# First layer of a two-layer decoder step: keys of the first sample batch during the prompt attention, difference-head norms by one root per 128 tokens

## What is computed

```python
diff = pb[:, :, 0] - lam * pb[:, :, 1]
ob = jnp.einsum('bhqk,bkhe->bqhe', diff.astype(vb.dtype), vb)
ob = rms_norm(ob, subln0) * (1.0 - LAMBDA_INIT)
return jnp.concatenate([oa.reshape(B, Q, -1), ob.reshape(B, Q, -1)], axis=-1)
```

## Time and profile before

| | us |
|---|---|
| median of three runs | 2104.91 (2103.43 to 2105.34) |
| the profiled execution's own time | 2101.7 |
| its span | 2099.8 |
| PE busy | 1811.7 (86%) |
| DVE busy | 992.5 (47%) |
| ACT busy | 565.1 (27%) |
| granted TensorE clock, mean | 0.91 |

### The profile page before, as it was taken

How to read it: one execution, slowest core, us unless ns; L and a number is a source line. 1 busy time by engine, 2 the same in 40 slices (tenths; PEclk the granted TensorE clock), 3 DMA queues, 4 the chain that set the end, 5 groups by cost and what they waited for, 6 DMA issues and landing times. The chain is left out here.

```text
span 2099.8 us, 30563 instructions
## 1 busy us (share of the span) xinstructions
PE 1811.7 (86%) x11582; PEld 1447.3 (69%) x11590; DVE 992.5 (47%) x1748; ACT 565.1 (27%) x1051; POOL 98.8 (5%) x89
## 2 busy tenths in 40 slices
PE   5998784888799999999989775666788999999999
PEld 4786452554479998899778632343446899789987
DVE  3456577444443222322246859998333422222222
ACT  3322352333322221122132331332222322112221
POOL 1312021000000000000001200000000000000000
PEclk8999896999899999999989955888789999999999
DMA  5232002999522322232215200000454222232221
GB/s 167 71 121 83 23 1 91 356 348 359 185 63 68 90 69 79 78 87 76 78 40 150 51 2 9 1 1 6 145 162 110 60 82 80 68 83 80 80 76 61
DMA packets 176381, 201.56 MB, mean 96 GB/s; under 512 B 21531, under 2 KB 130779, under 8 KB 176283
## 3 DMA queue, kind: packets, MB, share of 16 engines
q1 hardware_dynamic: 171242, 193.96, 28.9%
q10 hardware_dynamic: 4960, 6.05, 0.8%
q0 software_dynamic: 80, 0.26, 0.0%
HBM read 191.02 MB, written 9.22 MB: 95 GB/s over the span
## 5 line engine op out<-in xcount | busy, mean ns | idle before, releaser
L206 PE MATMUL ps<-feat_lo,w_hi 128*128 128x288 f32 x1408 | 418.7, 297 | 8.9 <-DVEq L1818 8.9
L208 PE MATMUL ps<-feat_hi,w_hi 128*128 128x288 f32 x1408 | 418.4, 297 | 0.0
L207 PE MATMUL ps<-feat_hi,w_lo 128*128 128x288 f32 x1408 | 418.2, 297 | 0.0
L188 DVE TENSOR_TENSOR w_lo<-w_raw,w_hi 128x2048 fp32r<-128x2048 f32 x96 | 220.1, 2293 | 386.2 <-ACT w_hi L182 386.1
L182 ACT ACTIVATE w_hi<-w_raw 128x2048 fp32r<-128x2048 f32 x96 | 183.8, 1914 | 366.4 <-PE ps L214 337.1
L206 PEld LDWEIGHTS ps<-feat_lo,w_hi 128*128 128x128 f32 x1408 | 267.4, 190 | 10.1 <-DVEq L1818 10.1
L207 PEld LDWEIGHTS ps<-feat_hi,w_lo 128*128 128x128 f32 x1408 | 267.5, 190 | 0.0
L208 PEld LDWEIGHTS ps<-feat_hi,w_hi 128*128 128x128 f32 x1408 | 267.3, 190 | 0.0
L206 PE MATMUL ps<-w_lo,feat_hi 128*128 128x512 f32 (+1 forms) x448 | 179.8, 401 | 18.7 <-DVE feat_lo L1707 9.4
L207 PE MATMUL ps<-w_hi,feat_lo 128*128 128x512 f32 (+1 forms) x448 | 176.4, 394 | 0.0
L208 PE MATMUL ps<-w_hi,feat_hi 128*128 128x512 f32 (+1 forms) x448 | 176.4, 394 | 0.0
(11 more groups left out here) (272 smaller groups left out, 2532.2 us busy)
## 6 DMA issues: line engine op xcount, KB each, us to landing
s_kslot<-in_cache_l_k_dram SPq DMA_DIRECT2D x64, 512.0 KB, 7.7
s_vslot<-in_cache_l_v_dram SPq DMA_DIRECT2D x64, 512.0 KB, 7.3
w_raw<-in_w_gate_dram SPq DMA_DIRECT2D x44, 512.0 KB, 4.0
w_raw<-in_w_up_dram SPq DMA_DIRECT2D x44, 512.0 KB, 5.2
w_raw<-in_w_in_dram SPq DMA_DIRECT2D x18, 1024.0 KB, 5.2
w_raw<-in_w_down_dram SPq DMA_DIRECT2D x16, 1024.0 KB, 5.0
s_kslot<-in_cache_l_k_dram SPq DMA_DIRECT2D x64, 128.0 KB, 2.2
s_vslot<-in_cache_l_v_dram SPq DMA_DIRECT2D x64, 128.0 KB, 2.6
```

Of the source, the lines that this page charges most:

```text
L188: dve.tensor_tensor(self.K.w_lo[:, n % 2, :], self.K.w_raw[:, n % 2, :], self.K.w_hi[:, n % 2, :].bitcast(F32), ALU.subtract).then_inc(sel ...
L206: pe.matmul(out, lhs[0], rhs[1], start=start, stop=False)
L207: pe.matmul(out, lhs[1], rhs[0], start=False, stop=False)
L208: return pe.matmul(out, lhs[0], rhs[0], start=False, stop=stop)
```

## The change

In the first layer only:

- `EarlyKeys`: SP loads the first batch's eight key pages while `a0` runs, into the space where `kt` will be (`kt0` over `feat_hi`, and `w_raw`). Its eight semaphores are `s0`'s `k_in`. To have semaphores enough, those of the earlier blocks are cleared by POOL at the start of `a0` and given back behind it.
- In `s0` the first batch's keys are turned out of that space, and the turned keys go to `vslot` (`kt_first`). So the first value pages wait until the first scores are done (`scored` at 4), and all eight of the second batch's key pages are asked for ahead of them instead of four.
- `HeadNorm` takes the place of both norms. ACT squares; PE multiplies 128 squared columns as the stationary operand by one column of ones, so that a sum per token lies in a partition (16 matmuls with one output column for the prompt); DVE scales 128 x 16 numbers, POOL takes the power -0.5, PE spreads each column back over 128 partitions (transpose of a broadcast column), and DVE applies it, reading PSUM. In `s0` the sums stand between the two halves of the first batch's units, the spreading and applying behind `scores(0)` and ahead of the loop. The sample heads' norm is done the same way inside `o0`: sums ahead of token tile 1, spreading ahead of tile 3; the sample columns are split after it.
- The block `sample_subln` is gone.

```diff
-def prompt_attention(nc, K, tag, q_at, k_at, v_at, gates, mask, mixed, sample_top=None):
+def prompt_attention(nc, K, tag, q_at, k_at, v_at, gates, mask, mixed, sample_top=None, early_keys=None, retired=()):
...
-        if any(mixed(p) for p in range(PAIRS)):
+        if retired or any(mixed(p) for p in range(PAIRS)):
             @block.gpsimd
             def _(pool):
+                for lo, hi in number_runs(retired):
+                    pool.sem_clear(range(lo, hi))
...
-        if sample_top is not None:
-            @block.sync
-            def _(sp):
+        @block.sync
+        def _(sp):
+            if early_keys is not None:
+                early_keys.load(sp)
+            if sample_top is not None:
                 sample_top.store(sp)
...
-class PromptSubln:
+class EarlyKeys:
+    def __init__(self, K, tag, cache_k):
+        self.K, self.cache_k = K, cache_k
+        self.k_in = [K.sem(f"{tag}_k_in_{j}") for j in range(N_PAGES)]
+        both = (K.kt0[:, :], K.w_raw.rearrange("p a n -> p (a n)"))
+        width = cache_k.shape[2]
+        self.pages = [both[j // 4][:, (j % 4) * width:(j % 4 + 1) * width] for j in range(N_PAGES)]
+    def load(self, sp):
+        for j in range(N_PAGES):
+            page = sp.value_load(self.K.pages[0:1, j:j + 1], min_val=0, max_val=self.cache_k.shape[0] - 1)
+            sp.dma_start(self.pages[j], self.cache_k[ds(page, 1), :, :].rearrange("a k d -> (a k) d"))\
+              .then_inc(self.k_in[j], 16)
+class HeadNorm:
+    def __init__(self, K, name, views, squares, sums, banks):
+        self.K, self.views, self.squares, self.banks = K, views, squares, banks
+        names = ("squared", "summed", "mean_ok", "rstd_ok", "spread", "normed")
+        self.S = {x: K.sem(f"{name}_{x}") for x in names}
+        self.n = len(views)
+        self.per = squares[0].shape[1] // P
+        self.sums = sums[:, 0:self.n * self.per]
+        self.norm = K.lams[:, 0:2, 0:self.n * self.per]
+    def square(self, act):
+        for k in range(self.n):
+            dst = self.squares[k]
+            if len(self.views[k].shape) == 3:
+                dst = dst.rearrange("p (h n) -> p h n", h=self.views[k].shape[1])
+            act.activation(dst, self.views[k], ACT.Square).then_inc(self.S["squared"], 1)
+    def sum_up(self, pe):
+        pe.wait_ge(self.S["squared"], self.n)
+        for k in range(self.n):
+            for x in range(self.per):
+                c = k * self.per + x
+                ins = pe.matmul(self.sums[:, c:c + 1], self.squares[k][:, x * P:(x + 1) * P], self.K.c("ones")[:, 0:1],
+                                start=True, stop=True)
+        ins.then_inc(self.S["summed"], 1)
+    def mean(self, dve):
+        dve.wait_ge(self.S["summed"], 1)
+        dve.tensor_scalar(self.norm[:, 0, :], self.sums, 1.0 / P, EPS, ALU.mult, ALU.add).then_inc(self.S["mean_ok"], 1)
+    def root(self, pool):
+        pool.wait_ge(self.S["mean_ok"], 1)
+        pool.tensor_tensor(self.norm[:, 1, :], self.norm[:, 0, :], self.K.c("minus_half")[:, 0:self.n * self.per],
+                           ALU.pow).then_inc(self.S["rstd_ok"], 1)
+    def bank(self, k):
+        return self.banks[k % len(self.banks)]
+    def spread(self, pe):
+        pe.wait_ge(self.S["rstd_ok"], 1)
+        for k in range(self.n):
+            if k >= len(self.banks):
+                pe.wait_ge(self.S["normed"], k - len(self.banks) + 1)
+            for x in range(self.per):
+                c = k * self.per + x
+                ins = pe.transpose(self.bank(k)[:, x * P:(x + 1) * P], self.norm[:, 1, c:c + 1].to_broadcast([P, P]),
+                                   self.K.c("ident"))
+            ins.then_inc(self.S["spread"], 1)
+    def apply(self, dve):
+        for k in range(self.n):
+            view, scale = self.views[k], self.bank(k)[:, 0:self.per * P]
+            if len(view.shape) == 3:
+                scale = scale.rearrange("p (h n) -> p h n", h=view.shape[1])
+            dve.wait_ge(self.S["spread"], k + 1)
+            dve.scalar_tensor_tensor(out=view, in0=view, scalar=self.K.subln_col8[:, 0:1], in1=scale,
+                                     op0=ALU.mult, op1=ALU.mult).then_inc(self.S["normed"], 1)
+    def done(self, eng):
+        eng.wait_ge(self.S["normed"], self.n)
...
+        subln, kt_first = None, kt
+        if early is not None:
+            kt_first = [vslot.rearrange("p j d -> p (j d)")[:, g * BANK * chunks:(g + 1) * BANK * chunks]
+                        .rearrange("p (c n) -> p c n", n=BANK) for g in range(2)]
+            halves = (pt.rearrange("p j n -> p (j n)"), probs[:, 0:PAST_LEN])
+            squares = [halves[h // 2][:, h % 2 * SEQ:(h % 2 + 1) * SEQ] for h in range(DIFF)]
+            subln = HeadNorm(K, "p_subln", [K.att[:, 4 + h, 0:SEQ] for h in range(DIFF)], squares,
+                             K.ps[:, 7, :], [K.ps[:, x, :] for x in (5, 6, 7)])
+
+        def is_first(b):
+            return early is not None and isinstance(b, int) and b == 0
...
-                    if subln is not None and isinstance(b, int) and b == 0:
-                        sp.wait_ge(subln.S["chain"], subln.STEPS)
                     sp.wait_ge(S["weighed"], b + 1)
                     sp.dma_start(vnew[:, :], new_v(b)).then_inc(S["new_v_in"], 16)
+                    if is_first(b):
+                        sp.wait_ge(S["scored"], 4)
...
-            load_k(0, ids, range(N_PAGES))
+            if early is None:
+                load_k(0, ids, range(N_PAGES))
             load_bias(0)
 
-
-            early = N_PAGES // 2 if chunks == KC else N_PAGES
             for b in range(LAST):
                 next_ids = page_ids(b + 1)
-                load_k(b + 1, next_ids, range(early))
+                ahead = N_PAGES // 2 if chunks == KC and not is_first(b) else N_PAGES
+                load_k(b + 1, next_ids, range(ahead))
                 load_v(b, ids, range(N_PAGES))
-                load_k(b + 1, next_ids, range(early, N_PAGES))
+                load_k(b + 1, next_ids, range(ahead, N_PAGES))
...
-                        ins = pe.transpose(K.ps[:, i % 2, x * P:(x + 1) * P], kslot[:, j, c * P:(c + 1) * P],
-                                           K.c("ident"))
+                        page = early.pages[j] if is_first(b) else kslot[:, j, :]
+                        ins = pe.transpose(K.ps[:, i % 2, x * P:(x + 1) * P], page[:, c * P:(c + 1) * P], K.c("ident"))
...
-            if subln is not None:
-                subln.tensor(pe)
             pe.sem_inc(S["turned_act"], half_units)
             pe.sem_inc(S["turned_dve"], half_units)
             pe.sem_inc(S["weighed"], 1)
             pe.sem_inc(S["scored"], 1)
             pe.sem_inc(S["o_read"], 1)
-            turn_k(0, range(len(units)))
+            turn_k(0, range(half_units))
+            if subln is not None:
+                subln.sum_up(pe)
+            turn_k(0, range(half_units, len(units)))
             scores(0)
+            if subln is not None:
+                subln.spread(pe)
+                subln.done(pe)
...
-                subln.scalar(act)
+                subln.square(act)
             act.sem_inc(S["kt_act"], 1)
...
-            keys(0, range(len(units)))
+            keys(0, range(half_units))
+            if subln is not None:
+                subln.mean(dve)
+            keys(0, range(half_units, len(units)))
+            if subln is not None:
+                subln.apply(dve)
...
-def sample_subln(nc, K):
+        heads = None
+        if subln:
+            square = mem.enter_context(nc.sbuf_tensor(f"{tag}_square", [P, DIFF * SAMP], F32))
+            heads = HeadNorm(K, f"{tag}_heads", [K.att[:, 4:8, SEQ:TOK]], [square[:, :]], K.ps[:, 7, :],
+                             [K.ps[:, 6, :]])
...
+                            if heads is not None and tile == tiles[0][0][0] and i == 0:
+                                if t == 1:
+                                    heads.sum_up(pe)
+                                if t == 3:
+                                    heads.spread(pe)
...
+            if heads is not None:
+                heads.square(act)
             if split:
                 for c in range(KC):
-                    act.activation(K.feat_hi[:, c, 0:TOK], K.att[:, c, :], ACT.Copy).then_inc(hi_ok, 1)
+                    act.activation(K.feat_hi[:, c, 0:SEQ], K.att[:, c, 0:SEQ], ACT.Copy).then_inc(hi_ok, 1)
+                if heads is not None:
+                    heads.done(act)
+                act.activation(K.feat_hi[:, :, SEQ:TOK], K.att[:, :, SEQ:TOK], ACT.Copy).then_inc(hi_ok, 1)
...
+                    if heads is not None and c == KC // 2:
+                        heads.mean(dve)
+                if heads is not None:
+                    heads.apply(dve)
+                    heads.done(dve)
+                dve.wait_ge(hi_ok, KC + 1)
...
+            retired, K.phase_sems = K.phase_sems, []
+            early = EarlyKeys(K, "s0", K.cache_l0_k)
             prompt_attention(
```

(52 more changed lines are left out.)

48 lines of the change are left out of this document (4 added, 44 removed).

## The result

The changed kernel takes **2069.99 us** (median of four runs, 2064.57 to 2073.30) and the kernel before, run beside it, 2104.17 (2100.80 to 2105.34): ratio 0.9838, 95% interval 0.9814 to 0.9862. The same kernel beside later experiments gave 2070.96, 2072.11 and 2071.01 us (0.9826, 0.9849, 0.9839), so the typical value is 2071. Its profiled execution took 2064.57 us (span 2062.5), 37.1 less than the one of before.

A forecast was written before the change was run, and what follows sets the result against it. PE was taken as the chain behind two holes, at the starts of `s0` and `o0`. Gains of 22.6 and 5.7 sum to 28.3 us: 2101.7 profiled becomes 2073.4, plus 3.2 for the median, 2076.6; range 2072 to 2083.

The forecast's parts named there:

- Term 1 to the loop's start: Start of `s0`: loop's first matmul at 359.9 in place of 382.70, 22.8 us gained, 22.6 after delay and clock.
- my high bound of 3.4: In `s0`: most the 16 narrow sums would take, in us, all at the low clock; 1.4 was forecast.
- Units and scores, with the clock's 0.7: In `s0` on PE: 15 units and scores 19.35 us, sixteenth unit 0.95; 0.7 comes back from less low clock.
- Spread and apply: In `s0` ahead of the loop: four transposes, four DVE applies and signals take 3.6 us, and PE waits for all.
- Power of 16 columns: In `s0` on POOL: 2.7 to 2.9 us, hidden behind the second half of the units and the scores.
- The late small step: First round of the `s0` loop: DVE's last small step comes 2.0 us into it, not 0.6, costing 0.9.
- the loop as before: `s0` loop: seven rounds of 23.5 us (one of 25.25) taken as unchanged but for the listed items.
- Term 2: Start of `o0`: PE starts at 563.97, not 570.27; 6.3 us gained, 0.6 off for extra sums and transposes, 5.7.
- Values late: Rival, chance 0.10: first batch's last value page comes 1.9 us late in round 1, perhaps 3; about 2079 us.
- a sign by which the prediction called itself wrong: First round of the `s0` loop: the prediction is wrong if PE waits for pages there; no size given.

The follow-up runs named there:

- Sqrt back: Changed kernel plus one unused ACT root of one column at the start of `s0`, ahead of the first key copies: 2079.76 us, 0.9881 of the kernel before.
- early keys only: Changed kernel with both old norms back (prompt norm's scratch in `kslot`, `sample_subln` its own block), first keys still early: 2114.24 us.
- The applies experiment: Changed kernel with the prompt norm's spreading and applying moved from ahead of the loop to behind it: 2071.37 us, beside 2070.96 for the changed kernel.

## Why the prediction was too small

The sign and the two main mechanisms were right, the sum was not.

- *Term 1 to the loop's start*: predicted 27.6 behind the block's start, 26.9 with the 0.7 of clock taken off; measured 27.86. That it is so near is partly luck, for two errors worked against each other. PE started 1.07 behind the block's start where I had 2.3: it was released by ACT's sequencer with the squares still running. The sums took 3.5 us and not 1.4, since each float32 product loads its weights twice and stands as two records: 32 for 16 sums. My row, eight transposes, has one load each. The score products show it too: 16 records for the eight matmuls of a bank. (So the sentence ahead of the prediction that float32 matmul rows count once per instruction does not hold for these.) Even my high bound of 3.4 was passed, at the high clock.
- *Units and scores, with the clock's 0.7*: 19.5 for 19.6. The clock was 0.81 from 336 to 345 and 1.00 from there to the end of round 1.
- *Spread and apply*: 3.8 (353.06 to 356.83) for 3.6. *Power of 16 columns*: 2.92, hidden, for 2.7 to 2.9.
- *The late small step* (0.9 off): it came 1.14 into the round, not 2.0. Round 1 took 0.5 more than the others (23.65), before 0.3 more, so it cost 0.2.
- **The step that failed: "the loop as before".** I took its rounds as unchanged but for these items, and so put the loop's own gain at nothing. B gave 3.6: 3.0 from the seven table loads, 1.7 because the trace of before had one round partly at the low clock, less 1.0 of a longer tail and the 0.2 of round 1. "ACT's exponentials then lose little, since its table and first copy come ahead of them" has the load in it, and the trace of before had it seven times. I never asked whether the removed root (L1229) was the reason it was there. With 3.0 more the forecast would have been 2073.6, and a range moved with it (2069 to 2080) would have held 2069.99.
- *The low round*: a round of 25.0 to 25.3 stands in all three traces that have the loads (before, Sqrt back, early keys only) and behind round 1 in none of the eleven without. So the 1.7 may belong to the loads as well; no run tests it.
- *Term 2*: PE 2.10 behind the last output, predicted 2.2; its extra sums and spreads cost 0.6, as predicted. POOL took 1.08 for two columns, not 0.7, and tile 4 still did not wait. DVE's three subtractions beside POOL took 1.89, 0.63 each, against 0.62 for the five before them, so they did not stand for it. (The bound of nine matmuls at twice 0.224 is 2.0, not 1.8; tile 0 took 4.57 against 4.69 before and gave nothing.)
- *Values late*: the forecast was no wait, with 1.4 us to spare. PE did not wait in the profiled execution, but nothing was to spare: its last weight loads of the product did.

```profile
366.94 0.16 PEld L1444 LDWEIGHTS ps<-s_vslot,s_pt 128*32 128x32 f32 x8 [0.49 <-DMA s_vslot<-in_cache_l_v_dram]
```

The product took 3.88 for 3.66; in the other three traces it took 3.83, 4.21 and 3.70, and in the second of these PE itself waited 0.34 for the last page. That is a sign by which the prediction called itself wrong, but at 0.3 us it is not what moved the total. The transfer was as estimated (13.6 us from the first request to the last page, 13.7 predicted), but the product came 10.4 behind the request and not 11.9. The applies experiment shows what follows when it comes 3.6 us earlier.
- *The remaining 3.6 us* from 2073.6 to 2069.99: 0.7 is the kernel before, 2104.17 beside the result and not 2104.91. Another 0.7 comes from the touched stages, which gave 32.0 where forecast and loads make 31.3. The other 2.2 lie in stages that the change does not touch. The four pairings of medians give 31.6 to 35.2 us. That is the spread over executions, and my range was too tight below for it: its 1.5 us was less than what the runs show.

## What to carry to other kernels

List what an edit removes by function table too: an activation with another table ahead of a loop can leave a load in the loop's body, and it is paid every round; look for loads in the loop and ask which operation put them there. Count weight loads by records of the same type of product, not by transposes. Before a block on the path is moved away, ask which transfer arrives during it, and price two linked parts together: here one part alone was slower.

## What the runs showed of the hardware

- The load of 1.28 us ran at the head of every round, though only copies and exponentials ran between two of them. Rounds with and without it differ by 0.36 to 0.47 us (changed kernel and Sqrt back, rounds at the full clock), and the next copy began at 384.11, 0.01 behind the load's end. The Trainium skill, ScalarE: Activation LUTs, section What ACT_TABLE_LOAD costs, gives some 1283 ns for the load, as here, and some 1380 ns of drain on top, which these rows do not show. The load at 334.47 shows none either, with ACT busy until just before it: the squares end at 334.46 and the root starts at 335.77, 1.31 in all. ScalarE activation tables: per-element evaluation and per-set limits, section Table sets in the compiler and the runtime (the Trainium skill too), says that loads are placed block by block; that agrees with a load in the loop's body that an operation ahead of the loop brings and takes away. What placed it there, no run shows.
- Among the narrow sums the granted clock fell from 1.00 to 0.50: in the kernel with doubled sums behind 32 of their records (16 took 1.93 us at 338.96 and 3.47 at 340.75), in the changed kernel's second trace between the two sets of 16 (1.91 us at 340.26, 3.56 at 342.03).
- The DMA queues moved 399 GB/s over round 1 of the changed kernel (values of one batch, keys of the next), with the DMA share at 1.01; before, 375. Both are above the 358 that the prediction quotes.
